# Four more weight slots for the experts, the overflow branch moved to their middle, and the forgetting attention as a pipeline over pairs of heads

## The chip, the cores and the metric

The kernel runs on one core of a Trainium2 chip. The metric is device time in microseconds (us); lower is better. "PE" is TensorE, "DVE" VectorE, "ACT" ScalarE, "POOL" GpSimd and "SP" the engine whose queue issues nearly all loads of weights.

## What is computed

Two transformer blocks over 256 tokens of width 1024, all in float32: first a mixer of latent attention and retention, cross attention to a memory, and a mixture of experts (MoE); then a mixer of forgetting attention ("fox") and pooling, a SwiGLU, an RWKV7 mixer and a second SwiGLU. The change touches the MoE and the fox mixer:

```python
# MoE: 32 experts, 2 of a chosen group of 8 per token
a = jnp.einsum('sd,edf->sef', hr, w_gate)
u = jnp.einsum('sd,edf->sef', hr, w_up)
act = jax.nn.silu(a) * u * gate[:, :, None].astype(hr.dtype)
return jnp.einsum('sef,efd->sd', act, w_down)
# fox: 8 heads of 64, query blocks of 128
logits = (jnp.einsum('bhqd,bhkd->bhqk', q_i, k).astype(jnp.float32) * scale
          + c_i[..., :, None] - cum[..., None, :])
p = jax.nn.softmax(jnp.where(causal, logits, -1e30), axis=-1)
return jnp.einsum('bhqk,bhkd->bhqd', p.astype(v.dtype), v)
# ... attn = attn * jax.nn.sigmoid(og), then concatenated with the pool and times w_out
```

## The kernel before, in words

The tokens are two tiles of 128. Each engine runs one straight program; semaphores join them. The PSUM banks are rings (`fill` on PE, `take` on the reader; a fill waits until its bank's last reader is done).

**Weights.** Every load of weights is a "unit" of up to 1 MB in a slot of 2048 floats per partition. SP issues the units strictly in the order in which the program lists them (`stream`, line 297 issues); before one goes out, SP waits until the unit that last held the slot has been used (`released`), and for slots outside `ring_w` also on a fence. There are 13 slots: 0 to 7 are `ring_w`, 8 to 12 lie in `work` from 12288.

**MoE.** Experts come in 8 quads of 4. A quad has 12 units: 4 gate, 4 up and 4 down matrices, 96 units in all, put into the slots in the turn 0-3, 8-12, 4-7. So unit n waits for the use of unit n-13. The fence of slots 8 and up is a transpose late in the cross attention. A chosen token is gathered into 32 places of its expert by a selection matrix (`Sel`, made by DVE, line 1571, for all 8 quads at once; `SelG`, line 1611, is the same times the gate). PE's order for quad q is: gate matmuls of q (line 1337), transposes and down matmuls of q-1 (1352), gather of q+1 (1388), transposes of `SelG` (1398), up matmuls of q (1337 again), scatter of q-1 (1409). Gate slots are free after the gate matmuls, up slots after the up matmuls, down slots after the down matmuls. ACT applies SiLU (1236) and copies the down result (1488); DVE multiplies and adds the scatter to the residual X (1602).

**Overflow.** If an expert got more than 32 tokens, a branch computes the rest densely. PE, ACT, DVE and SP each read a flag and jump over that branch; it stands after the last quad (for SP after the last expert unit is issued). It isn't taken with these inputs.

**Into fox.** `rounded_linear` computes the 2568 columns of `w_fin` in three passes of rounded halves. ACT makes the high half of each unit (`part_high_act`, line 503, 1.9 us a unit), DVE the low half (line 512). ACT does units 0 and 1, normalises token tile 0 (lines 414, 420, with POOL at 425 and 426), does units 2 and 3, normalises tile 1. PE warms up (line 462), transposes tile 0 (441), computes column block 0 of tile 0, transposes tile 1, and goes on.

**Fox attention.** PE computes the scores of all 8 heads (lines 1906, 1908); DVE adds decay and mask (2057) and takes the row maximum by pairs (2062, 2063); ACT takes the exponential by head (1972); PE transposes the probabilities by head (1915), ACT copies them out; then PE computes all outputs with the probabilities stationary and v moving (1924 to 1927), DVE divides by the row sum (2071) and multiplies by the sigmoid gate (2074), PE transposes the result (1933), ACT copies it into `mixT`, and the output projection `w_out2` starts (341). The constant table comes in two loads at the start (lines 578, 592); its `decay` part is last used by the retention (`ro`).

## Time and profile before

| | |
|---|---|
| median of 3 runs | 1367.98 us (1365.78 to 1368.43) |
| profiled execution, its own time | 1374.08 us |
| its span | 1372.2 us |
| PE busy in the span | 1222.1 us (89%) |
| DVE, ACT, POOL busy | 735.2, 247.9, 94.3 us |
| mean granted TensorE clock | 0.946 |
| DMA | 247.25 MB, mean 180 GB/s |

Times below are us from the start of the span. The MoE lies between about 305 and 548, the fox mixer between 548 and 702. In a timeline row the bracket says how long the engine had been idle before and what ended that. "issue" is time in which the engine waited for nothing that the profile shows. PEclk is the granted clock as a share of 2.4 GHz.

### The profile page before, as it was taken

To read this page: it belongs to the slowest core of one execution; us is meant where nothing else is said; L and a number is where in the kernel's file an instruction comes from. 1 tells how busy PE (TensorE), PEld (TensorE's weight loads), DVE (VectorE), ACT (ScalarE), POOL (GpSimd) and SP (SyncE) were. 2 spreads that over 40 slices of the span, in tenths; PEclk is the share of its full clock that TensorE was granted. 3 is DMA by queue.
4 is the path that set the end of the run, shared out by engine and by line. 5 is a ranking of instruction groups with operands and counts; after the bars stand their busy time and mean duration, and the time that the engine had idled before them with its cause. 6 is when DMAs were issued, how large, how long until landed. Compare 5 with 4: busy or idle time off the path is not lost.

```text
span 1372.2 us, 20894 instructions
## 1 busy us (share of the span) xinstructions
PE 1222.1 (89%) x9023; PEld 880.1 (64%) x9023; DVE 735.2 (54%) x1178; ACT 247.9 (18%) x427; POOL 94.3 (7%) x86
## 2 busy tenths in 40 slices
PE   5999998998666668898899999989999898999997
PEld 4855645555333333587558888766769884688886
DVE  5447412142111111555188777677876657777774
ACT  5413111210000001523210000135331100100000
POOL 1010000000000000120000000000110431000000
PEclk9999999999888878999799999999999999999999
DMA  9643243167999999350465553136300224855500
GB/s 345 230 169 123 87 157 123 41 239 308 402 390 408 402 383 394 120 176 1 158 230 185 187 187 127 34 86 223 110 2 4 65 65 161 269 184 184 185 31 31
DMA packets 106338, 247.25 MB, mean 180 GB/s; under 512 B 8113, under 2 KB 56256, under 8 KB 93826
## 3 DMA queue, kind: packets, MB, share of 16 engines
q1 hardware_dynamic: 106052, 245.71, 49.2%
q8 instruction: 73, 1.20, 0.4%
q0 software_dynamic: 144, 0.15, 0.0%
q14 instruction: 23, 0.19, 0.0%
q10 hardware_dynamic: 46, 0.01, 0.0%
HBM read 244.80 MB, written 1.05 MB: 179 GB/s over the span
## 4 chain that ended last, share of the span: by engine, by line
PE 80%; DMA 10%; DVE 4%; ACT 2%; SPq 2%; issue 2%; POOL 0%; DVEq 0%
PE bank L479 13%; PE bank L478 13%; PE bank L480 13%; DMA ring_w<-expert_w_gate 8%; PE bank L341 8%; PE bank L327 6%; PE bank L2332 4%; PE bank L1337 3%; PE bank L1352 2%; SPq L297 1%; PE bank L462 1%; PE bank L2226 1%; PE bank L441 1%; DMA work<-expert_w_down 1%; PE bank L1747 1%
## 5 line engine op out<-in xcount | busy, mean ns | idle before, releaser
L478 PE MATMUL bank<-work_rounded,work_rounded 128*128 128x512 f32 (+2 forms) x704 | 278.1, 395 | 6.8 <-DVE work_rounded L1681 5.2
L480 PE MATMUL bank<-work_rounded,work_rounded 128*128 128x512 f32 (+2 forms) x704 | 275.1, 391 | 0.0
L479 PE MATMUL bank<-ring_w_rounded,work_rounded 128*128 128x512 f32 (+2 forms) x576 | 228.1, 396 | 0.0
L478 PEld LDWEIGHTS bank<-work_rounded,work_rounded 128*128 128x128 f32 x704 | 133.1, 189 | 37.5 <-issue 3.9
L480 PEld LDWEIGHTS bank<-work_rounded,work_rounded 128*128 128x128 f32 x704 | 132.8, 189 | 27.9
L479 PEld LDWEIGHTS bank<-ring_w_rounded,work_rounded 128*128 128x128 f32 x576 | 110.0, 191 | 23.3 <-issue 0.2
L341 PE MATMUL bank<-ring_w,work 128*128 128x512 f32 x256 | 113.4, 600 | 2.6 <-ACT work L1143 1.4
L1681 DVE TENSOR_TENSOR ring_w_rounded<-ring_w,work_rounded 128x1024 fp32r<-128x1024 f32 x84 | 102.9, 1225 | 2.9
L1337 PE MATMUL bank<-ring_w,work 128*32 128x256 f32 x768 | 71.2, 459 | 35.1 <-DMA ring_w<-expert_w_gate 33.0
L1236 ACT ACTIVATE work<-bank 128x256 f32<-128x256 f32 x52 | 20.1, 386 | 406.7 <-PE bank L480 340.3
L341 PEld LDWEIGHTS bank<-ring_w,work 128*128 128x128 f32 x256 | 48.5, 193 | 60.8 <-issue 57.4
L327 PE MATMUL bank<-ring_w,work 128*128 128x512 f32 x192 | 83.5, 593 | 0.9 <-DVE work L451 0.9
L1595 DVE TENSOR_TENSOR work<-bank,cols 128x512 f32<-128x512 f32 x16 | 11.0, 691 | 134.0 <-PE bank L1388 134.0
L479 PE MATMUL bank<-work_rounded,work_rounded 128*128 128x512 f32 x192 | 74.9, 390 | 0.0
L1337 PEld LDWEIGHTS bank<-ring_w,work 128*32 128x32 f32 x768 | 36.4, 131 | 57.4 <-issue 47.6
L1681 DVE TENSOR_TENSOR work_rounded<-work,work_rounded 128x1024 fp32r<-128x1024 f32 (+1 forms) x56 | 64.4, 1149 | 1.9
L327 PEld LDWEIGHTS bank<-ring_w,work 128*128 128x128 f32 x192 | 36.3, 190 | 45.2 <-issue 44.0
L425 POOL TENSOR_SCALAR stat<-stat 128x1 f32<-128x1 f32 (+3 forms) x21 | 7.6, 360 | 767.1 <-ACT work L414 663.4
L1680 DVE CAST work_rounded<-bank 128x256 fp32r<-128x256 f32 x44 | 18.7, 424 | 75.2 <-PE bank L1747 75.2
L1337 PE MATMUL bank<-work 128*32 128x256 f32 x256 | 32.9, 453 | 29.2 <-DMA ring_w<-expert_w_gate 29.2
L1680 DVE CAST work_rounded<-ring_w 128x1024 fp32r<-128x1024 f32 x84 | 57.5, 684 | 0.0
L813 ACT COPY work<-bank 128x512 f32<-128x512 f32 (+3 forms) x53 | 28.3, 559 | 143.1 <-PE bank L480 68.1
(445 smaller groups left out, 1830.6 us busy)
## 6 DMA issues: line engine op xcount, KB each, us to landing
ring_w<-expert_w_gate SPq DMA_DIRECT2D x26, 1024.0 KB, 13.8
ring_w<-expert_w_up SPq DMA_DIRECT2D x22, 1024.0 KB, 19.8
ring_w<-ffn_w_down SPq DMA_DIRECT2D x22, 1024.0 KB, 5.0
work<-expert_w_down SPq DMA_DIRECT2D x20, 1024.0 KB, 9.1
ring_w<-expert_w_down SPq DMA_DIRECT2D x12, 1024.0 KB, 10.5
work<-ffn_w_gate SPq DMA_DIRECT2D x12, 1024.0 KB, 5.5
work<-ffn_w_up SPq DMA_DIRECT2D x12, 1024.0 KB, 8.2
work<-expert_w_up SPq DMA_DIRECT2D x10, 1024.0 KB, 11.5
```

The costliest lines, as they stand in the source:

```text
L327: mm = nc.tensor.matmul(ps[:, 0:w_], lhsT[:, kk, t * P:(t + 1) * P], wv[kk // step][:, kk % step, :], start=kk == 0, stop=kk == kt - 1)
L341: mm = nc.tensor.matmul(ps[:, :], lhsT[:, k, t * P:(t + 1) * P], wv[k // 4][:, k % 4, :], start=k == 0, stop=k == KD - 1)
L478: nc.tensor.matmul(out, lhsT[0], rhs[0], start=first, stop=False)
L479: nc.tensor.matmul(out, lhsT[0], rhs[1], start=False, stop=False)
L480: return nc.tensor.matmul(out, lhsT[1], rhs[0], start=False, stop=last)
L813: nc.scalar.copy(dst, ps[:, 0:dst.shape[1]] if len(dst.shape) == 2 else ps[:, 0:dst.shape[1] * dst.shape[2]].rearrange("p (a b) -> p a b", ...
L1236: nc.scalar.activation(sil[:, i % 2], ps[:, 0:FF], ACT.Silu).then_inc(sem(f"silu_{u}"), 1)
L1337: mm = nc.tensor.matmul(ps[own, i * FF:(i + 1) * FF], hg[:, q % 2, k, own], units_[j][:, k, :], start=k == 0, stop=k == KD - 1)
L1352: mm = nc.tensor.matmul(banks[c][own, :], actT[:, q % 2, k, own], wd[j][:, k, c * 512:(c + 1) * 512], start=k == 0, stop=k == 1)
L1680: links["dve"](nc.vector.tensor_copy(high, value))
L1681: return nc.vector.tensor_tensor(low, value, high.bitcast(F32), ALU.subtract).then_inc(done, 1)
L2332: mm = nc.tensor.matmul(ps[w, h * HD:(h + 1) * HD], lhs(w, 8 * half + h), rhs(w, 8 * half + h), start=True, stop=True)
```

## The change

Four slots are added: 13 and 14 in `work` at 6144 and 8192 (where `Sel` and `SelT` of all quads lay), 15 and 16 over `decay`, `pool` and `sel` of the constant table. The turn becomes 15, 16, 0-3, 8-14, 4-7, so unit n waits for unit n-17. `Sel`, `SelG` and `SelT` shrink to two quads each and are made as the quads go, two ahead. `pool` and `sel` (1.3 MB) are no longer loaded at the start but as `late_const`, after the `w_fin` units. The overflow branch moves to before quad 4 (`MIDDLE`) on PE, ACT and DVE, and for SP to after the last unit of quad 3; ahead of it PE finishes quad 3. At the start of fox, ACT makes the high half of unit 0 only, then normalises tile 0, then does units 1, 2, 3, then tile 1. The fox attention is interleaved by pairs of heads: probabilities are divided by the row sum before they are transposed, v is stationary and the transposed probabilities move, so the output comes out transposed, and the gate is transposed before its sigmoid (`ogT`). Its core:

```diff
-        SLOT, SLOTS, MORE = 2048, 8, 5
+        SLOT, SLOTS, MORE = 2048, 8, 9
...
             if slots[0] < SLOTS:
                 name, base, at = "ring_w", ring_w, slots[0] * SLOT
+            elif slots[0] < 13:
+                name, base, at = "work", work, EXTRA + (slots[0] - SLOTS) * SLOT
+            elif slots[0] < 15:
+                name, base, at = "work", work, 6144 + (slots[0] - 13) * SLOT
             else:
-                name, base, at = "work", work, EXTRA + (slots[0] - SLOTS) * SLOT
+                name, base, at = "const", const, CONST["decay"][0] + (slots[0] - 15) * SLOT
...
+                if (slots[0] >= SLOTS and name != "late_const") or name.startswith("f1"):
+                    late = fence.get(name.split(".")[0], ()) if slots[0] < 15 else ("ro.1",)
...
-        n_const1 = CONST["invf"][1]
+        n_const1, n_const2 = CONST["decay"][1], CONST["sel"][1]
...
-            sp.dma_start(const[:, n_const1:], A["const_table"][:, n_const1:]).then_inc(sem("const2_in"), 16)
+            sp.dma_start(const[:, n_const2:], A["const_table"][:, n_const2:]).then_inc(sem("const2_in"), 16)
...
-        Sel = view(6144, T, NE, CAP)
-        SelT = view(8192, NQ, S)
-        SelG = view(22528, T, NE, CAP)
+        Sel = [view(22528 + 256 * i, T, EPQ, CAP) for i in range(2)]
+        SelG = [view(23040 + 256 * i, T, EPQ, CAP) for i in range(2)]
+        SelT = [view(23552 + 256 * i, S) for i in range(2)]
...
-            turn = itertools.cycle((0, 1, 2, 3, 8, 9, 10, 11, 12, 4, 5, 6, 7))
+            turn = itertools.cycle((15, 16, 0, 1, 2, 3, 8, 9, 10, 11, 12, 13, 14, 4, 5, 6, 7))
...
+            def second_half(q):
+                tr_pe(pe, "moe", q, pick=lambda k: slice(k, FF, 2))
+                down_quad_pe(pe, q)
             for q in range(NQ + 1):
+                if q == MIDDLE:
+                    second_half(q - 1)
+                    scatter(q - 1)
+                    overflow_pe(pe)
                 if q < NQ:
                     await_moved(pe, f"hg.{q}.1")
                     ps = fill(pe, "GU", f"moe.gu.{q}")
                     gu_quad_pe(pe, q, 0, ps)
-                if q:
-                    tr_pe(pe, "moe", q - 1, pick=lambda k: slice(k, FF, 2))
-                    down_quad_pe(pe, q - 1)
+                if q and q != MIDDLE:
+                    second_half(q - 1)
                 if q + 1 < NQ:
                     gather(q + 1)
                 if q < NQ:
                     turn_scatter(q)
                     gu_quad_pe(pe, q, 1, ps)
-                if q:
+                if q and q != MIDDLE:
                     scatter(q - 1)
-            drained(pe, "GU", "TT", "Z")
-            drained(pe, "Y")
-            if "O" in phases:
-                overflow_pe(pe)
+            drained(pe, "GU", "TT", "Z", "Y")
...
+            def select(q):
+                if q >= 2:
+                    peek(dve, f"hg.{q - 2}.1")
+                V.tensor_tensor(Sel[q % 2], slots_of(key, q), each, ALU.is_equal).then_inc(sem("selected"), 1)
+            def weigh(q):
+                dve.wait_ge(sem("selected"), q + 1)
+                if q >= 2:
+                    peek(dve, f"selT.{q - 2}")
+                V.tensor_tensor(SelG[q % 2], Sel[q % 2], slots_of(gate, q), ALU.mult).then_inc(sem("gated"), 1)
+            select(0)
+            select(1)
...
+                if q == MIDDLE:
+                    add_scatter(q - 1)
+                    overflow_dve(dve)
                 if q + 1 < NQ:
                     take_gather(q + 1)
                 if q < NQ:
+                    if q + 2 < NQ:
+                        dve.wait_ge(sem("gated"), q + 1)
+                        select(q + 2)
+                    if q + 1 < NQ:
+                        weigh(q + 1)
                     ps = take(dve, "Z", f"selT.{q}")
-                    V.tensor_copy(SelT[:, q], ps[:, 0:S]).then_inc(moved["Z"], 1)
+                    if q >= 2:
+                        peek(dve, f"x.{q - 2}.1.1")
+                    V.tensor_copy(SelT[q % 2], ps[:, 0:S]).then_inc(moved["Z"], 1)
                     step_dve(dve, "moe", q)
-                if q:
+                if q and q != MIDDLE:
                     add_scatter(q - 1)
...
+            place("late_const", (15, 16), [(A["const_table"][:, n_const1:n_const2], const[:, n_const1:n_const2])])
...
+            def pair_outputs(p):
+                ps = fill(pe, "D", f"foT.{p}")
+                for i in range(2):
+                    h, own = 2 * p + i, slice(i * HD, (i + 1) * HD)
+                    await_moved(pe, f"fprT.{h}")
+                    nc.tensor.matmul(ps[own, 0:S], v(0, h), fprT[:, h, 0:S], start=True, stop=False)
+                    mm = nc.tensor.matmul(ps[own, P:S], v(1, h), fprT[:, h, S:3 * P], start=False, stop=True)
                 mm.then_inc(full["D"], 1)
-            for h in range(FH):
-                pe.wait_ge(sem("fexp"), 2 * h + 2)
-                ps = fill(pe, "A", f"fprT.{h}")
-                for b in range(3):
-                    mm = nc.tensor.transpose(ps[:, b * P:(b + 1) * P], fsc[:, h, b * P:(b + 1) * P], ident)
-                mm.then_inc(full["A"], 1)
-            await_moved(pe, f"fprT.{FH - 1}")
-            v = lambda t, h: fproj[:, t, 2 * FW + h * HD:2 * FW + (h + 1) * HD]
-            for t in range(T):
-                ps = fill(pe, "D", f"fo.{t}")
-                for h in range(FH):
-                    o = slice(h * HD, (h + 1) * HD)
-                    if t == 0:
-                        mm = nc.tensor.matmul(ps[:, o], fprT[:, h, 0:P], v(0, h), start=True, stop=True)
-                    else:
-                        nc.tensor.matmul(ps[:, o], fprT[:, h, P:S], v(0, h), start=True, stop=False)
-                        mm = nc.tensor.matmul(ps[:, o], fprT[:, h, S:3 * P], v(1, h), start=False, stop=True)
-                mm.then_inc(full["D"], 1)
-            for t in range(T):
-                pe.wait_ge(sem("fgated"), t + 1)
-                ps = fill(pe, "A", f"foT.{t}")
-                for k in range(4):
-                    mm = nc.tensor.transpose(ps[:, k * P:(k + 1) * P], fo[:, t, k * P:(k + 1) * P], ident)
-                mm.then_inc(full["A"], 1)
+            pair_scores(0)
+            pair_scores(1)
+            pair_turned(0)
+            pair_scores(2)
+            pair_outputs(0)
+            pair_turned(1)
+            pair_scores(3)
+            for p in range(1, 4):
+                pair_outputs(p)
+                if p < 3:
+                    pair_turned(p + 1)
...
-            out_linear(pe, "w_out2", mixT, lambda t: await_moved(pe, f"foT.{t}"), lambda: norm_pe(pe, "f0", tiles=(0,)))
+            out_linear(pe, "w_out2", mixT, lambda t: await_moved(pe, "foT.3"), lambda: norm_pe(pe, "f0", tiles=(0,)))
...
-            if "C" in phases:
-                peek(act, f"selT.{NQ - 1}")
             part_high_act(act, "w_fin", 0)
-            part_high_act(act, "w_fin", 1)
             def ready(t):
                 if t:
-                    part_high_act(act, "w_fin", 2)
-                    part_high_act(act, "w_fin", 3)
-                if "C" in phases:
-                    await_moved(act, f"x.{NQ - 1}.1.{t}")
+                    peek(act, f"x.{NQ - 1}.1.1")
+                    for n in (1, 2, 3):
+                        part_high_act(act, "w_fin", n)
+                await_moved(act, f"x.{NQ - 1}.1.{t}")
...
-            await_moved(act, "w_fin.3.0", "w_fin.3.1")
-            og = fproj[:, :, OG:OG + FW]
-            nc.scalar.activation(og, og, ACT.Sigmoid).then_inc(sem("fgate"), 1)
...
-                if h:
-                    copy_chunk_act(act, f"fprT.{h - 1}", fprT[:, h - 1])
-            copy_chunk_act(act, f"fprT.{FH - 1}", fprT[:, FH - 1])
-            for t in range(T):
-                ps = take(act, "A", f"foT.{t}")
-                nc.scalar.copy(mixT[:, 0:4, t * P:(t + 1) * P], ps[:, :].rearrange("p (k n) -> p k n", k=4)).then_inc(moved["A"], 1)
+            act.wait_ge(sem("fss"), T)
+            for t in range(T):
+                ps = take(act, "A", f"ogT.{t}")
+                nc.scalar.activation(gateT[:, :, t * P:(t + 1) * P], ps[:, :].rearrange("p (k n) -> p k n", k=4),
+                                     ACT.Sigmoid).then_inc(moved["A"], 1)
...
+                if p:
+                    pair_turned_act(p - 1)
...
             part_low_dve(dve, "w_fin", 0)
+            norm_split_dve(dve, "d", "mix_norm_2", 0)
             part_low_dve(dve, "w_fin", 1)
-            norm_split_dve(dve, "d", "mix_norm_2", 0)
             part_low_dve(dve, "w_fin", 2)
...
+            def pair_probs_dve(p):
+                pair = slice(2 * p, 2 * p + 2)
+                dve.wait_ge(sem("fexp"), 4 * p + 4)
+                L(V.reciprocal(fst[:, 6:8, pair], fst[:, 6:8, pair]))
                 for t, (lo, hi) in enumerate(((0, P), (P, 3 * P))):
-                    last = V.scalar_tensor_tensor(fsc[:, h, lo:hi], ps[:, lo:hi], cum[:, t, h:h + 1], C("cmask")[:, lo:hi],
-                                                  ALU.add, ALU.add)
-                last.then_inc(moved["D"], 1)
-                if h % 2:
-                    await_moved(dve, f"fscore.{h}")
-                    L(V.tensor_reduce(fst[:, 4, h - 1:h + 1], fsc[:, h - 1:h + 1, 0:P], AX.X, ALU.max, negate=True))
-                    V.tensor_reduce(fst[:, 5, h - 1:h + 1], fsc[:, h - 1:h + 1, P:], AX.X, ALU.max, negate=True) \
-                        .then_inc(sem("fnmax"), 1)
-            dve.wait_ge(sem("fexp"), 2 * FH)
-            L(V.reciprocal(fst[:, 6:8, 0:FH], fst[:, 6:8, 0:FH]))
-            dve.wait_ge(sem("fgate"), 1)
-            for t in range(T):
-                ps = take(dve, "D", f"fo.{t}")
-                v = fo[:, t].rearrange("p (h d) -> p h d", h=FH)
-                V.tensor_tensor(v, ps[:, :].rearrange("p (h d) -> p h d", h=FH), bc(fst[:, 6 + t, 0:FH], HD, 2),
-                                ALU.mult).then_inc(moved["D"], 1)
-                await_moved(dve, f"fo.{t}")
-                V.tensor_tensor(fo[:, t], fo[:, t], fproj[:, t, OG:OG + FW], ALU.mult).then_inc(sem("fgated"), 1)
+                    V.tensor_tensor(fsc[:, pair, lo:hi], fsc[:, pair, lo:hi], bc(fst[:, 6 + t, pair], hi - lo, 2),
+                                    ALU.mult).then_inc(sem("fprob"), 1)
+            def pair_gated_dve(p):
+                ps = take(dve, "D", f"foT.{p}")
+                V.tensor_tensor(mixT[:, p, :], ps[:, 0:S], gateT[:, p, :], ALU.mult).then_inc(moved["D"], 1)
+            pair_scores_dve(0)
+            pair_scores_dve(1)
+            pair_probs_dve(0)
+            pair_scores_dve(2)
+            pair_probs_dve(1)
+            await_moved(dve, "ogT.1")
+            pair_gated_dve(0)
+            pair_scores_dve(3)
+            pair_probs_dve(2)
+            pair_gated_dve(1)
+            pair_probs_dve(3)
+            pair_gated_dve(2)
+            pair_gated_dve(3)
...
-        add_swiglu("E", "f0", 0, lambda act: after_residual(act, "w_out2"), ("fmixed.1", "fo.1"),
+        add_swiglu("E", "f0", 0, lambda act: after_residual(act, "w_out2"), ("fmixed.1", "foT.3"),
...
-            cut = unit_at[f"moe.d.{NQ - 1}.{EPQ - 1}"] + 1 if "C" in phases and "O" in phases else 0
+            cut = unit_at[f"moe.d.{MIDDLE - 1}.{EPQ - 1}"] + 1 if "C" in phases and "O" in phases else 0
```

## Rows read from the trace of the kernel before

**Rows 1.** Waits of PE over the whole span: us in total, times, longest
```profile
PE bank L1337 <- DMA ring_w<-expert_w_gate: 62.2, 7, 10.8
PE bank L462 <- issue: 8.0, 1, 8.0
```
**Rows 2.** The chain that ended last, in order of time: start us, us, what
```profile
315.17 10.35 DMA ring_w<-expert_w_gate
...
527.79 10.09 DMA work<-expert_w_down
538.13 5.34 PE bank L1352 x32
547.29 8.00 issue
```
**Rows 3.** Timeline of SP's issues: start us, us from first issue to last, group
```profile
221.39 8.55 SPq L297 DMA_DIRECT2D ring_w<-expert_w_gate  x4
269.40 2.41 SPq L297 DMA_DIRECT2D work<-expert_w_up  x4
...
285.33 30.27 SPq L297 DMA_DIRECT2D ring_w<-expert_w_gate  x4
...
529.55 56.38 SPq L297 DMA_DIRECT2D ring_w<-hy_w_in  x11
```
**Rows 4.** Windows in the MoE: stretch, busy us by engine, PEclk, DMA share, GB/s
```profile
399.00:400.00 1.00, 1.00 (x16) 0.22 (x8) 0.00 (x0) 0.38 (x1) 0.00 (x0) 1.00 0.31 115
400.00:401.00 1.00, 1.00 (x10) 0.67 (x7) 0.00 (x0) 0.54 (x1) 0.00 (x0) 1.00 0.14 57
...
314.00:540.00 226.00, 156.69 (x1516) 85.48 (x1512) 35.59 (x62) 14.23 (x30) 0.00 (x0) 0.84 0.96 393
...
404.00:424.00 20.00, 11.53 (x112) 5.42 (x114) 4.20 (x7) 0.38 (x1) 0.00 (x0) 0.79 1.01 425
```
**Rows 5.** Timeline of PE in the MoE: start us, us, line, shape
```profile
310.61 3.66 PE L1337 MATMUL bank<-ring_w,work 128*32 128x256 f32 x64 [1.96 <-issue]
314.20 3.84 PE L1388 MATMUL bank<-work 128*128 128x128 f32 x32
...
343.14 3.89 PE L1409 MATMUL bank<-work 128*128 128x512 f32 x8
356.99 5.55 PE L1337 MATMUL bank<-ring_w,work 128*32 128x256 f32 x64 [9.95 <-DMA ring_w<-expert_w_gate]
```
**Rows 6.** Timeline of DVE, ACT and PE from the last expert into the fox part
```profile
547.33 0.69 DVE L1602 TENSOR_TENSOR X<-X,bank 128x512 f32<-128x512 f32 x1 [0.17 <-PE bank L1409]
...
549.72 3.70 ACT L503 CAST work_rounded<-ring_w 128x2048 fp32r<-128x2048 f32 x2 [5.61 <-issue]
...
556.72 1.15 ACT L420 ACTIVATE work<-X,stat 128x1024 f32<-128x1024 f32 x1 [2.25 <-POOL stat L426]
...
567.87 1.03 PE L441 MATMUL bank<-const,work 128*128 128x128 f32 x8
```
**Rows 7.** Timeline of PE and DVE in the fox attention
```profile
640.71 0.60 PE L1906 MATMUL bank<-work 128*128 128x256 f32 x2
...
659.09 3.68 PE L1924 MATMUL bank<-work 128*128 128x64 f32 x16 [0.57 <-ACT work L813]
...
671.10 1.12 PE L1933 MATMUL bank<-const,work 128*128 128x128 f32 x4 [0.66 <-DVE work L2074]
...
648.85 1.53 DVE L2057 SCALAR_TENSOR_TENSOR work<-bank,work,const 128x128 f32<-128x128 f32 x4
650.41 0.42 DVE L2062 TENSOR_REDUCE work<-work 128x2 f32<-128x256 f32 x1
650.87 0.69 DVE L2063 TENSOR_REDUCE work<-work 128x2 f32<-128x512 f32 x1
```
**Rows 8.** Windows of the fox attention, columns as in Rows 4
```profile
635.00:640.00 5.00, 1.55 (x11) 1.26 (x10) 3.70 (x6) 0.00 (x0) 0.00 (x0) 1.00 0.01 3
...
655.00:660.00 5.00, 3.61 (x14) 2.42 (x14) 0.25 (x1) 3.41 (x13) 0.00 (x0) 0.50 0.00 0
```

More of the change, by code:

```diff
@@ L78, in _constants @@
     parts["sel"] = sel.reshape(P, -1)
+    parts["tri"] = (i[:, None] <= i[None, :]).astype(float)
+    parts["ones"] = np.ones((P, P))
     blk = i // CH
@@ L1569, in moe_dve @@
             each = slot_key.unsqueeze(1).unsqueeze(1).to_broadcast([P, T, EPQ, CAP])
-            for q in range(NQ):
-                V.tensor_tensor(quad(Sel, q), slots_of(key, q), each, ALU.is_equal).then_inc(sem("selected"), 1)
+            def select(q):
[9 more added lines that the diff above has]
+            select(1)
             V.tensor_copy(place_of, by_tile).then_inc(moved["D"], 1)
@@ L1608, in moe_dve @@
                                   bc(gate8[:, t], G, 1), ALU.mult))
-            dve.wait_ge(sem("selected"), NQ)
-            for q in range(NQ):
-                V.tensor_tensor(quad(SelG, q), quad(Sel, q), slots_of(gate, q), ALU.mult).then_inc(sem("gated"), 1)
+            weigh(0)
             await_moved(dve, "rank", "count")
@@ L1929, in fox_pe @@
[L1929 to L1934 removed]
+            for t in range(T):
+                ps = fill(pe, "A", f"ogT.{t}")
+                for k in range(4):
+                    mm = nc.tensor.transpose(ps[:, k * P:(k + 1) * P], fproj[:, t, OG + k * P:OG + (k + 1) * P], ident)
+                mm.then_inc(full["A"], 1)
@@ new lines, in fox_pe, with pair_scores @@
+            await_moved(pe, "fT.1.1")
+            def pair_scores(p):
+                for h in (2 * p, 2 * p + 1):
+                    ps = fill(pe, "D", f"fscore.{h}")
+                    for t, (lo, hi) in enumerate(((0, P), (P, 3 * P))):
+                        nc.tensor.matmul(ps[:, lo:hi], fqz[:, h, t * P:(t + 1) * P], fkT[:, h // 2, 0:hi - lo],
+                                         start=True, stop=False)
+                        mm = nc.tensor.matmul(ps[:, lo:hi], C("sel")[:, h * P:(h + 1) * P], ncumT[:, 0:hi - lo],
+                                              start=False, stop=True)
+                    mm.then_inc(full["D"], 1)
```

131 lines of the change are left out of this document (74 added, 57 removed).

## Prediction, before the changed kernel was run

> **What bounds the kernel now.** I read the waits of PE first. Seven waits of the expert gate matmuls for their weights make 62.2 us, and one single wait of 8.0 us at line 462 is put down to "issue" [rows 1]; nothing else on PE comes near. The chain in order of time puts both on the path that sets the end: transfers of expert weights (first row at 315.17), the last expert transfer until 537.9, its down matmuls, the scatter, and then 8.00 us in which nothing runs [rows 2]. So the MoE is bound by DMA, and the rest of the kernel by PE.
>
> Next, why the transfers take so long. The SP timeline shows four gate units at 221.39, nothing until the fence opens at 269.40, and a group of four that begins at 285.33 and ends 30.27 us later: its last three wait until quad 0's gate matmuls end at 314.27 [rows 3, 5]. So 13 units are there when the MoE begins and 83 are not. In the windows a stretch without holes moves 425 GB/s, while 399 to 401 moves 115 and 57, and the whole of 314 to 540 averages 393 [rows 4]. 226 us at 393 GB/s is 88.8 MB; at 425 this would take 209 us. So about 17 us of it are holes, some 2.4 us in each of seven quads. They come from the slots: the down units of quad q sit where those of q-1 sat (n-13), and these are freed only by the down matmuls of q-1, which PE does after the gate matmuls of q. When gate q lands, only up q (4 units, 4 x 2.47 = 9.9 us, 1.049 MB at 425 GB/s being 2.47 us) is queued; gate matmuls 5.55 [rows 5], transposes, ACT's copy and down matmuls take about 11 together.
>
> **Part 1: four slots more.** (a) 17 units are there before the MoE, 79 are not: 4 x 2.47 = 9.9 us less to move while PE waits. Slots 15 and 16 have an open fence, slots 8 to 14 open at 269.40: seven units and then the ring's four are 11 x 2.47 = 27.2 us, in by 297, before the first gate matmuls at 310.61 [rows 3, 5]. (b) With n-17, the down units of q wait for gate q-1 and up q-1, and gate q+1 for up q-1 and down q-1. When gate q lands, nine units (22 us) are queued, and down q-1 ends after 11: no hole. For the ramp: from 314.3, units 17 to 20 go out at once (10 us), the next four after up 0, near 322, the next after down 0, near 332; each comes before the one ahead is through. PE needs per quad 5.5 gate, 5.3 down, 3.8 gather, 3.7 up, 3.9 scatter [rows 2, 5] and about 1 of transposes, 23 us of the 29.6 that 12 units take, so PE doesn't become the bound. Sum: 9.9 + 17 = 27 us at best. I take 25.5, since a hole at the ramp or in the middle may remain. The floor is (a) with a third of the holes closed, 15 us; the ceiling adds about 1 us because DVE makes 2 selections instead of 8 ahead of the first gather's copy, 28 us.
>
> The Trainium skill, "DMA: Bandwidth & Descriptors", section Specifications, says that HBM gives one core some 358 GB/s. By that the 79 units would take 231 us and this part would lose time instead of gaining. The trace speaks against it for this kernel: 425 GB/s over 20 us [rows 4].
>
> The new waits in DVE's loop (selections of q+2 behind gather q, `SelT` behind the scatter of q-2) cost two short operations per quad, beside DVE that is idle most of the MoE (35.59 us busy of 226 [rows 4]): nothing. If PE ever waited for them it would be under 1 us a quad. The two constant parts that go later (1.3 MB, 3 us of queue) stand behind `w_fin` and are needed 65 us after it begins; they push the pool and output weights by 3 us, which lie ready for tens of us. SP issues one load more: nothing. At the start PE has no wait that this load ends: nothing.
>
> **Part 2: the branch leaves the end.** Before, the scatter ends at 547.3 and PE's next matmul is 8.00 us later [rows 2]; ACT loses 5.61 and then makes two high halves (3.70) before the normalisation [rows 6]. After: ACT ends its copy of the down result near 544.1 and does high half 0 until 546.0, tile 0 of X is complete at 546.1, square 1.2, POOL 2.25, scale 1.15 [rows 6]: transposes at 550.9 where they were at 558.9, 8 us gained. Then it gives some back: ACT does three high halves (5.6) instead of two ahead of tile 1, and DVE one low half (2.3) more inside the critical part. Tile 1 is normalised at 561.0; PE ends column block 0 at about 560.1 and waits 0.9. Its transposes of tile 1 start at 561 where they were at 567.87 [rows 6]: 6.5 us net. Ceiling 8; floor 3, if DVE's low halves (2.3 each) let PE wait once more.
>
> The branch isn't gone: in the middle PE finishes quad 3 and then loses the same 8 us. From the landing of down 3 (T): down 5.3, copy, scatter 3.9, branch 8, gate 4 until about T+23, gather and up 4 until T+32; gate 5 lands at T+39.6. The nearest slot that depends on gate 4 is wanted at T+42. So it is covered, with 7 us to spare.
>
> **Part 3: the fox attention.** Before, it goes from 638.85 (scores) to 672.2 (output projection). PE: a head's scores 1.3 us, as a 128x256 product takes 0.43 from start to start at full clock [rows 7]; outputs 10.2 us, at half clock. In the pipeline the loop is DVE scores of p (after PE's last head: 0.75 of 1.53, then 0.42 and 0.69 [rows 7]), DVE division (no such row; as reductions of the same sizes, plus the reciprocal, 1.5), PE transposes of p-1 (0.9), PE scores of p+1 (2.6), DVE again: 2.1 + 1.5 + 0.9 + 2.6 = about 7.3 with hops, twice after 646.2, so the last scores stand at 660.8. Two more divisions, ACT's exponentials and copies, transposes and the last output pair end near 669 at full clock. Output pairs with v stationary are 2 x (0.43 + 0.22) = 1.3 us; the row of the old form, 3.68 for 16, bounds it from above at 2.6 [rows 7]. But PE will wait about half the time. In the row 635 to 640 it was busy 1.55 of 5 us and the clock stayed at 1.00 (2.4 GHz); in 655 to 660, after a stretch of waits, it was 0.50 (1.2 GHz) [rows 8]. At half clock from 655 on, scores, transposes and outputs double and the end is 676. Between 669 and 676 I take 671: 1 us gained (bounds +3 and -4). The gate's transposes fill PE's wait for DVE before 638.85 and ACT's two sigmoids come well before the first exponential: nothing; without that cover 2 us.
>
> **Sum:** 25.5 + 6.5 + 1 = 33 us. The profiled execution took 1374.08 us (span 1372.2), 6.1 above the median of 1367.98; it becomes 1341, and the median 1335.
>
> **Rivals.**
> A. The holes stay in part: PE's releases come late again (half-clock matmuls, or SP's queue doesn't take 13 units ahead), and only the head start and a few us are won. For it: SP waits in order, one late slot holds up all behind. Against: nine units of cover. 11 + 5 + 0 = 16: 1352 us.
> B. The branch in the middle shows. SP also jumps there, and while it does, nothing is issued; PE loses its 8 us while it already has the reordered quad. Against: at SP's end-of-MoE jump only about 1.4 us passed before the first `w_fin` unit at 529.55 [rows 3], and 11 units are in flight then. Price 8: 1343 us. The Trainium skill, "Runtime: NRT & Kernel Launch", section Instruction fetch mechanics, says that a jump outside the fetched pages stalls for a fetch; it would put such a stall on every engine with the branch.
> C. The fox pipeline is slower than the old order (half clock from 650, every hop exposed): it loses 5 us instead of gaining 1, so 1341 us.
> D. Slower than before: PE stays at half clock through the whole MoE, because it never gets a long busy stretch. Then a quad is gate 5.5, up 5.5, down 5.3, gather 7.5, scatter 7.7, transposes 2: 34 us against 31.8 now and 29.6 of DMA. PE is then the bound, from any quad cost over 29.6 on; it decides the sign only over about 35, including a branch and hops. At 36, 8 x 4.2 = 34 lost and 7 won elsewhere: 1395 us. Against: the mean clock of 314 to 540 is 0.84 with longer waits than the new ones [rows 4].
> E. The change doesn't do what it says, say a fence holds slots 13 to 16: then part 2 and 3 alone, 1360 us.
>
> **Chances.** Forecast 0.70, A 0.13, B 0.05, C 0.05, D 0.03, E 0.04. A measurement of this kernel can tell 0.2% (2.7 us) from no change. Faster needs over 2.7 of the 33 us: all but D, a bad A and a bad E: 0.94; within 0.2%: 0.02; slower: 0.04. The three ceilings, 28 + 8 + 3 = 39 us, give 1329; I go 4 us beyond, for terms set to nothing that may give something (1325). Upward the range ends at A's 1352, which leaves out D, E and the worse half of A.
>
> **What would show it.** Right: 17 expert units issued before the first gate matmul; windows of 420 to 425 GB/s without a hole from 315 to about 510; PE's waits on expert weights of about 7 us each; last expert unit landed near 511; an "issue" wait of 8 us between quads 3 and 4 and none at line 462; gap from landing to tile 1's transposes 23 instead of 30 us; from fox's first score to the output projection about 32 us. Wrong: a period per quad above 30.5 us, PE waiting on DVE's selections, or a granted clock of 0.5 in most of the fox attention.

## The result, and the profile after

The changed kernel takes **1336.49 us** (median of 4 runs; three of them lie between 1335.52 and 1336.51, the fourth, 4686.64 us, was disturbed), the kernel before 1368.2 us beside it (1365.78 to 1370.8, 4 runs). The ratio is **0.9766, 95% interval 0.9743 to 0.9788**: 31.7 us less. The forecast was 1335.0 in a range of 1325 to 1352.

| | before | after |
|---|---|---|
| profiled execution, its own time | 1374.08 us | 1335.52 us |
| its span | 1372.2 us | 1333.7 us |
| PE busy | 1222.1 us | 1201.3 us |
| mean granted TensorE clock | 0.946 | 0.967 |
| DMA | 247.25 MB | 247.27 MB |

Both spans are cut here at the same five places: the first gate matmul, the last down matmuls (their weights have then landed), tile 1's transposes, the first fox score and the first matmul of `w_out2`. All later experiments are cut at these places too.

| stage, us | before | after | less |
|---|---|---|---|
| start to first gate matmul | 310.6 | 306.7 | 3.9 |
| MoE, to the landing of the last weights | 227.5 | 206.8 | 20.7 |
| to the transposes of tile 1 | 29.7 | 22.3 | 7.4 |
| `w_fin`, to the first fox score | 71.0 | 71.5 | -0.5 |
| fox attention, to `w_out2` | 33.2 | 30.5 | 2.7 |
| `w_out2` to the end | 700.2 | 695.8 | 4.4 |

The four stages in the middle give 30.3 us. In the first and the last stage I know of nothing that the change could shorten, and yet they differ by 8.3; the experiments come back to this.

**The MoE.** The longer waits of PE from 300 to 540: us in total, times, longest. They answer to [rows 1].

```profile
PE bank L1342 <- DMA work<-expert_w_gate: 21.2, 3, 9.0
PE bank L1342 <- DMA ring_w<-expert_w_gate: 16.1, 2, 8.6
PE bank L1342 <- issue: 9.1, 3, 7.5
...
PE bank L1357 <- DMA work<-expert_w_down: 3.6, 1, 3.6
PE bank L466 <- DVE X L1627: 1.0, 1, 1.0
```

Seven waits of 62.2 us are now five waits of 37.3, about 7.5 each, and the wait at the warm-up matmuls (line 466, which was 462) went from 8.0 to 1.0. The "issue" wait of 7.5 is the branch in its new place. Next, windows with columns as in [rows 4]:

```profile
310.00:514.00 204.00, 150.94 (x1508) 81.89 (x1504) 39.45 (x71) 14.23 (x30) 0.00 (x0) 0.88 1.01 415
325.00:345.00 20.00, 15.70 (x150) 9.06 (x146) 5.56 (x10) 0.97 (x2) 0.00 (x0) 0.91 1.01 422
...
405.00:425.00 20.00, 13.92 (x162) 8.66 (x162) 2.81 (x6) 0.38 (x1) 0.00 (x0) 0.83 1.01 411
...
485.00:505.00 20.00, 12.17 (x152) 5.99 (x156) 0.91 (x2) 1.54 (x3) 0.00 (x0) 0.83 1.02 422
```

The last two columns are DMA share and GB/s. No stretch looks like the two rows of 115 and 57 GB/s of before: the transfers run through, and eight of the nine 20 us windows from 325 to 505 lie between 419 and 422. That is a little under the 425 of [rows 4]. The Trainium skill, "DMA: Bandwidth & Descriptors", section Measured, gives 425 GB/s for a long load while the other core of the pair is idle, beside the lower limit of its Specifications; the rows here side with the measured figure.

SP's timeline (start, us from first issue to last, group) shows the head start; it answers to [rows 3]:

```profile
196.88 1.11 SPq L301 DMA_DIRECT2D const<-expert_w_gate  x2
218.60 0.81 SPq L301 DMA_DIRECT2D ring_w<-expert_w_gate  x2
226.34 0.81 SPq L301 DMA_DIRECT2D ring_w<-expert_w_up  x2
266.62 0.81 SPq L301 DMA_DIRECT2D work<-expert_w_up  x2
267.47 2.63 SPq L301 DMA_DIRECT2D work<-expert_w_down  x4
270.14 0.46 SPq L301 DMA_DIRECT2D work<-expert_w_gate  x1
274.43 8.07 SPq L301 DMA_DIRECT2D ring_w<-expert_w_gate  x3
282.56 0.42 SPq L301 DMA_DIRECT2D ring_w<-expert_w_up  x1
310.45 0.81 SPq L301 DMA_DIRECT2D const<-expert_w_up  x2
...
501.99 52.14 SPq L301 DMA_DIRECT2D ring_w<-hy_w_in  x11
```

2 + 2 + 2 + 2 + 4 + 1 + 3 + 1 = 17 units go out before the MoE, and the 18th at 310.45, when quad 0's gate matmuls (306.74 to 310.40) end.

**The branch.** PE in the middle of the MoE:

```profile
397.57 3.89 PE L1414 MATMUL bank<-work 128*128 128x512 f32 x8
408.92 0.65 PE L1342 MATMUL bank<-ring_w,work 128*32 128x256 f32 x3 [7.46 <-issue]
...
432.62 5.84 PE L1342 MATMUL bank<-work 128*32 128x256 f32 x64 [8.98 <-DMA work<-expert_w_gate]
```

The stall stands between the scatter of quad 3 and the gate matmuls of quad 4, and PE still waits 9.0 us for the weights of quad 5: the stall is covered with 9 us to spare (7 were forecast). The chain in order of time at the end of the MoE, answering to [rows 2, 6]:

```profile
485.06 28.26 DMA work<-expert_w_down
513.57 6.31 PE bank L1357 x32
519.88 1.93 PE bank L1414 x4
...
522.55 1.16 ACT work L418 x2
...
525.70 5.49 ACT work_rounded L507 x3
...
534.63 1.16 ACT work L424
535.84 1.09 PE bank L445 x8
```

Landing, down matmuls, half a scatter, normalisation: the one idle time of size between them is an "issue" wait of 1.04 us on ACT, before its high halves. Tile 0's transposes start 12.9 us after the landing (526.48 in PE's timeline; 20.7 before), tile 1's 22.3 after it. The gap narrows again because of ACT's three high halves (5.49), as forecast.

**The fox attention.** PE's and DVE's timelines, answering to [rows 7]:

```profile
617.69 1.29 PE L1961 MATMUL bank<-const,work 128*128 128x128 f32 x6 [3.16 <-DVE work L2125]
...
626.01 0.87 PE L1961 MATMUL bank<-const,work 128*128 128x128 f32 x6 [2.35 <-DVE work L2125]
...
632.66 0.87 PE L1961 MATMUL bank<-const,work 128*128 128x128 f32 x6 [2.35 <-DVE work L2125]
```

```profile
616.60 1.03 DVE L2125 TENSOR_TENSOR work<-work 128x256 f32<-128x256 f32 x2
621.58 0.74 DVE L2113 SCALAR_TENSOR_TENSOR work<-bank,work,const 128x128 f32<-128x128 f32 x2 [3.95 <-PE bank L1952]
...
628.23 0.74 DVE L2113 SCALAR_TENSOR_TENSOR work<-bank,work,const 128x128 f32<-128x128 f32 x2 [1.94 <-PE bank L1952]
```

They read as a loop between the two engines: PE idles 3.16 and 2.35 us until DVE has divided, then transposes and computes the next scores, and DVE idles 3.95 and 1.94 us until it has those. From one transposes row to the next 8.3 and 6.7 us pass (7.3 was forecast). And the clock did not fall far. These are the whole attention before and after, and the same of a kernel of experiment 2 with the same attention (columns as in [rows 4]):

```profile
638.85:672.01 33.16, 28.01 (x144) 24.59 (x145) 13.11 (x29) 10.89 (x41) 0.00 (x0) 0.73 0.03 7
```

```profile
607.35:637.88 30.53, 21.44 (x121) 17.28 (x121) 16.34 (x40) 11.51 (x41) 0.00 (x0) 0.89 0.00 0
```

```profile
612.55:645.75 33.20, 24.43 (x120) 19.38 (x121) 16.34 (x40) 11.60 (x41) 0.00 (x0) 0.79 0.00 0
```

In the old form PE was busy 28.0 of 33.2 us at a mean clock of 0.73, and from 655 on, in slices of 5 us, the clock was 0.50 ([rows 8] has the first). The pipeline has PE busy for 21.4 us, idle for 9.1, and at a mean clock of 0.89; in slices of 5 us it never shows less than 0.66. How long the pipeline takes goes with that clock: 28.6 to 28.8 us at 0.94 (four traces), 30.5 at 0.89 (two), 33.2 at 0.79 (one).

### The profile page after: what moved, and what is told of

Same layout as the page of the kernel before. It is cut to its first block, busy times and chain, and to the rows that moved or that the text cites. A ratio compares the mean times of both kernels' runs of the same rounds, so it can differ in the third digit from the quotient of the medians.

```text
span 1333.7 us, 20901 instructions
## 1 busy us (share of the span) xinstructions
PE 1201.3 (90%) x9007; PEld 860.1 (64%) x9007; DVE 737.7 (55%) x1189; ACT 246.7 (18%) x426; POOL 93.4 (7%) x86
## 2 busy tenths in 40 slices
DMA packets 106484, 247.27 MB, mean 185 GB/s; under 512 B 8130, under 2 KB 56273, under 8 KB 93971
## 4 chain that ended last, share of the span: by engine, by line
PE 75%; DMA 9%; DVE 9%; ACT 3%; SPq 2%; issue 2%; POOL 1%; DVEq 0%
PE bank L483 13%; PE bank L482 13%; PE bank L484 13%; PE bank L345 8%; PE bank L331 6%; DMA work<-expert_w_gate 5%; PE bank L2402 4%; PE bank L1342 3%; DMA work<-expert_w_down 2%; PE bank L1357 2%; SPq L301 2%; DMA ring_w<-expert_w_gate 1%; PE bank L1393 1%; PE bank L445 1%; PE bank L1084 1%
## 5 line engine op out<-in xcount | busy, mean ns | idle before, releaser
L1342 PE MATMUL bank<-ring_w,work 128*32 128x256 f32 x512 | 52.3, 431 | 32.3 <-DMA ring_w<-expert_w_gate 16.1
L1342 PEld LDWEIGHTS bank<-ring_w,work 128*32 128x32 f32 x512 | 26.4, 123 | 50.9 <-issue 44.1
L1342 PE MATMUL bank<-work 128*32 128x256 f32 x384 | 39.0, 443 | 13.3 <-DMA work<-expert_w_gate 13.3
```

The lines of the kernel that those rows point to most:

```text
L1342: mm = nc.tensor.matmul(ps[own, i * FF:(i + 1) * FF], hg[:, q % 2, k, own], units_[j][:, k, :], start=k == 0, stop=k == KD - 1)
```

## The experiments

The kernels of the first four experiments were run in one set (kernel before in it: 1367.77 us, 9 runs), the next four in a second (1366.59, 11 runs), the last three in a third (1371.3, 11 runs). Ratios are to the kernel before of the same set.

**1. Only 13 slots again, everything else kept.**

```diff
-            turn = itertools.cycle((15, 16, 0, 1, 2, 3, 8, 9, 10, 11, 12, 13, 14, 4, 5, 6, 7))
+            turn = itertools.cycle((0, 1, 2, 3, 8, 9, 10, 11, 12, 4, 5, 6, 7))
```

> The changed kernel with the old turn of 13 slots; all else of the change stays. If the slots bring the gain of the MoE by a head start of four units (9.9 us) and by closing the holes of some 2.4 us a quad (17 us at most), this kernel takes back 21 to 27 us: 1358 to 1363 us, with holes again in the stream and a last expert unit that lands 21 to 27 us later than in the changed kernel. If only the head start counts, it is 10 us slower: 1346 us.

Measured: 1358.43 us, ratio 0.9939 (0.9912 to 0.9966). Waits of PE, and a window of the kernel with 13 slots:

```profile
PE bank L1342 <- DMA ring_w<-expert_w_gate: 54.4, 6, 10.9
...
340.00:500.00 160.00, 106.07 (x1024) 57.00 (x1022) 28.94 (x52) 9.66 (x20) 0.00 (x0) 0.84 0.98 403
```

The holes are back (403 GB/s), and the MoE takes 224.9 us. By the medians the four slots are worth 1358.4 - 1336.5 = 22 us, by the MoE stage of the two traces 224.9 - 206.8 = 18.1; 57 to 69% of the whole gain. That the head start alone counts (1346 us) is ruled out.

**2. 15 slots: without the two in the constant table.**

```diff
-            turn = itertools.cycle((15, 16, 0, 1, 2, 3, 8, 9, 10, 11, 12, 13, 14, 4, 5, 6, 7))
+            turn = itertools.cycle((0, 1, 2, 3, 8, 9, 10, 11, 12, 13, 14, 4, 5, 6, 7))
```

> The changed kernel with 15 slots (the two over the constant table unused). The slot theory counts what is queued when gate q lands: 7 units, 17 us, against 11 us until the down matmuls of q-1 are done, so no hole is left, and only two units of the head start are lost: 5 us slower, 1341 to 1342 us, with DMA at 420 GB/s throughout. If each slot gives an equal share, it loses half of what 13 slots lose: 11 to 13 us, 1348 us.

Measured: 1341.35 us, ratio 0.981 (0.9776 to 0.9843), MoE 210.5 us. Its window, and the same of the changed kernel:

```profile
340.00:500.00 160.00, 107.53 (x1022) 57.79 (x1020) 28.47 (x51) 9.63 (x20) 0.00 (x0) 0.84 1.01 420
```

```profile
340.00:500.00 160.00, 113.65 (x1102) 60.96 (x1106) 27.47 (x49) 10.00 (x21) 0.00 (x0) 0.85 1.01 420
```

So 15 slots already close the holes, and the last two bring only their head start: 4.9 us by the medians, 3.7 in the stage, for two units of 2.5. The steps are 17 us for slots 13 and 14 (14.4 in the stage) and 5 for slots 15 and 16. By my estimate from this step, a further slot would be worth about 2.5 us; no run has one.

**3. The branch back at the end, everything else kept.**

```diff
             for q in range(NQ + 1):
-                if q == MIDDLE:
-                    second_half(q - 1)
-                    scatter(q - 1)
-                    overflow_pe(pe)
...
             drained(pe, "GU", "TT", "Z", "Y")
+            overflow_pe(pe)
```

(the same on ACT and DVE, and for SP behind the last expert unit)

> The changed kernel with the overflow branch back after the last quad, on all four engines. If its 8 us of issue time stand on the path there and are hidden in the middle: 6.5 to 8 us slower, 1343 to 1344.5 us, and the issue wait of 8 us is again ahead of line 466. If the end of the MoE is set by ACT and POOL anyway: under 3 us slower.

Measured: 1339.29 us, ratio 0.9794 (0.9754 to 0.9835; 4 runs). PE's timeline has the stall where it was:

```profile
512.12 5.34 PE L1357 MATMUL bank<-work 128*32 128x512 f32 x32 [2.03 <-DMA work<-expert_w_down]
517.39 3.89 PE L1414 MATMUL bank<-work 128*128 128x512 f32 x8
529.30 2.93 PE L466 MATMUL bank<-const 128*128 128x512 f32 x3 [8.03 <-issue]
```

From landing to tile 1's transposes 29.9 us pass instead of 22.3: the 7.6 of the theory. The time, though, rose by 2.8 only, less than the 6.5 to 8 expected, with wide intervals. That number is the rival's (under 3 us), but the rival's reason, that ACT and POOL set the end of the MoE anyway, does not fit the 7.6 us in the stage. Experiment 10 repeats it.

**4. No branch at all.** Since it isn't taken with these inputs, nothing that runs is left out but the reading of the flag and the jump.

```diff
         def overflow(eng, body):
-            eng.wait_ge(sem("flags"), 1)
-            some = eng.value_load(flags[0:1, 0:1], min_val=0, max_val=1)
-            with eng.If(some > 0):
-                body()
+            return
```

> The changed kernel without the overflow branch at all (with these inputs the branch isn't taken, so nothing is left out that runs). If the branch in the middle is fully hidden by the transfers: no change, 1335 to 1337.5 us. If it shows: up to 8 us faster, 1328.5 us.

Measured: 1336.35 us (4 runs from 1333.05 to 1343.04), ratio 0.9792 (0.9746 to 0.9838), MoE 205.4 us against 206.8, and against 205.5 in a second trace of the changed kernel (experiment 9). PE in the middle of it:

```profile
398.65 0.42 PE L1342 MATMUL bank<-ring_w,work 128*32 128x256 f32 x3
...
428.11 5.16 PE L1342 MATMUL bank<-work 128*32 128x256 f32 x64 [16.19 <-DMA work<-expert_w_gate]
```

PE goes on at once behind the scatter (398.65, no idle time in front), and then waits 16.2 us for quad 5 instead of 9.0. The stall was a part of a wait: the wait is longer by 7.2 us where the stall of 7.46 is gone. In the middle the branch costs nothing that these runs can show.

**5. The old fox attention in the changed kernel.** All of the fox part on PE, ACT and DVE is as before; slots, branch and order of the halves are as after.

```diff
-            pair_scores(0)
-            pair_scores(1)
-            pair_turned(0)
...
+            for h in range(FH):
+                ps = fill(pe, "D", f"fscore.{h}")
...
-            out_linear(pe, "w_out2", mixT, lambda t: await_moved(pe, "foT.3"), lambda: norm_pe(pe, "f0", tiles=(0,)))
+            out_linear(pe, "w_out2", mixT, lambda t: await_moved(pe, f"foT.{t}"), lambda: norm_pe(pe, "f0", tiles=(0,)))
```

> The changed kernel with the forgetting attention in the old order (all scores, all transposes, all outputs, division and gate at the end). The forecast's term for the pipeline is 1 us, the two traces say 2.7 us from the first score to the output projection (33.2 against 30.5): 1337.5 to 1339 us. If the pipeline is worth its full-clock sum: 1339.5 us; if it costs time at half clock: 1333 us.

Measured: 1340.7 us, ratio 0.9799 (0.9772 to 0.9826). The attention takes 34.8 us against 30.5, 4.3 less in the pipeline. In the whole time it is 4.2 by the medians and 3.6 by the means of these six runs and of nine of the changed kernel, all but the one of 4686.64 (1340.8 and 1337.2), somewhat more than expected. In the old order PE's timeline has the outputs of all heads in one block, behind the last head's exponential and copy. The clock is 1.00 from 613 to 623 and 0.50 from 628 on, so this block and the transposes behind it run at half clock:

```profile
630.09 3.67 PE L1961 MATMUL bank<-work 128*128 128x64 f32 x16 [0.57 <-ACT work L817]
```

**6. The scores two pairs ahead.** If the ring of hops between PE and DVE is the limit, PE has to compute the scores of pair 2 before it waits for the division of pair 0.

```diff
             pair_scores(1)
-            pair_turned(0)
             pair_scores(2)
+            pair_turned(0)
             pair_outputs(0)
-            pair_turned(1)
             pair_scores(3)
+            pair_turned(1)
```

> The changed kernel with PE's order in the fox pipeline altered: scores of pair 2 before the transposes of pair 0, scores of pair 3 before the transposes of pair 1. In the changed kernel DVE waits 3.95 us for the scores of pair 2 and 1.94 us for those of pair 3, since PE first waits for the probabilities. If that hop bounds the pipeline: 5 to 7 us from the first score to the output projection, 1330 to 1331.5 us. If DVE or ACT bound it, or the clock does: under 2 us.

Measured: 1332.94 us, ratio 0.9733 (0.9704 to 0.9763). The attention takes 23.9 us: 6.6 less, as the theory said. PE's waits for the divided probabilities (us in total, times, longest), in the changed kernel and in this one, give 6.3 of it:

```profile
PE bank L1961 <- DVE work L2125: 7.9, 3, 3.2
```

```profile
PE bank L1961 <- DVE work L2125: 1.6, 2, 1.0
```

The median fell by 3.6 only, to above the 1330 to 1331.5 expected; see experiment 11.

**7. The same, with six filler matmuls of 256 columns in PE's waits, to hold the clock.**

```diff
+            FILL = (2, 2, 2, 0)
...
+                        for _ in range(FILL[p]):
+                            nc.tensor.matmul(ps[:, 0:256], ident, const[:, 0:256], start=True, stop=True)
```

> As scores_ahead, and PE fills its waits for the probabilities with two idle products of 128x256 each before the transposes of pairs 0 to 2. If the half clock in this stage costs time once the order is right: 1 to 3 us faster than scores_ahead. If PE is busy enough by then, or its time is covered by DVE: no change, or up to 1 us slower where a product runs into the wait's end.

Measured: 1332.15 us, ratio 0.9726 (0.9696 to 0.9757): 0.8 below experiment 6, well inside the intervals. The attention takes 24.7 us. The mean granted clock of the attention is 0.93 in both, and 1.00 behind its first 5 us, so there was no low clock for the fillers to lift. They are not worth having.

**8. The kernel before once more, for its trace.** Its one run of 1368.24 us has a span of 1366.4.

> The kernel before, unchanged, for a second trace of it. The first trace was 6 us above the median and differs from the changed kernel's by 3.9 us before the first gate matmuls, where the change does next to nothing. If that is the variation of single executions, this trace has its first gate matmuls at 305 to 311 us and a span of 1362 to 1372 us, and its MoE and fox stages as long as in the first trace (227.5 and 33 us, within 3 us).

| stage, us | before | again | after | 3 | 4 | 1 | 2 |
|---|---|---|---|---|---|---|---|
| to the first gate matmul | 310.6 | 308.6 | 306.7 | 306.4 | 303.9 | 305.0 | 309.7 |
| MoE | 227.5 | 225.1 | 206.8 | 205.7 | 205.4 | 224.9 | 210.5 |
| fox attention | 33.2 | 33.2 | 30.5 | 28.8 | 28.7 | 30.5 | 33.2 |
| `w_out2` to the end | 700.2 | 699.2 | 695.8 | 698.0 | 699.7 | 699.3 | 700.2 |

(The numbers in the head are those of the experiments.) The second trace came out as expected, but its MoE is 2.4 us shorter than in the first, so against it the slots gain 18.3 us in the stage and not 20.7. The MoE follows the slots. The first stage varies from 303.9 to 309.7 among kernels whose PE program is the same there, and the last from 695.8 to 700.2. So the 3.9 and 4.4 us of these stages in the first table can't be told from that variation. The fox attention as a pipeline also takes 28.6 to 33.2 in single traces: over the seven traces that have it (experiments 9 and 10 below among them) the mean is 29.9, against 33.7 over the three of the old form (33.2, 33.2, 34.8), 3.8 us less.

**9, 10, 11. Changed kernel, branch at the end and scores ahead, once more side by side.** They are to settle the two places where a trace shows 7 us and the medians of two sets about 3.

> The changed kernel as it is, measured beside the next two on one chip, because the first medians were taken in two batches and lie within each other's intervals. Theory: 1335 to 1338 us, ratio to the kernel before 0.976 to 0.978. In its trace the MoE phase is 206 to 208 us and the fox attention 30.5; what differs from the first trace lies before the first gate matmul or behind the fox attention.

> The changed kernel with the overflow branch back at the end of the experts. Theory of the branch (it costs 7.5 us at the end and nothing in the middle): 7 to 8 us slower than after_again of this batch, 1343 to 1345. Rival (the stall is partly made up later, so that less than half is left, as the first median of 1339.3 suggests): 2 to 4 us slower. Both theories expect the 8 us issue wait at line 466 in the trace; they differ in the time alone.

> The changed kernel with the scores of pairs 2 and 3 ahead of the transposes of pairs 0 and 1. Theory of hops (6.6 us shorter fox attention, and nothing given back): 5.5 to 7 us faster than after_again of this batch, 1329 to 1331. Rival (half is given back after the attention, as the 3 us longer rest of the first trace suggests): 3 to 4 us faster, and the phase behind the attention again about 3 us longer than that of after_again.

| | us, median (6 runs) | ratio, interval | landing to tile 1 | fox | `w_out2` to end |
|---|---|---|---|---|---|
| 9, changed kernel | 1337.99 | 0.976, 0.9719 to 0.9802 | 21.1 | 28.6 | 700.5 |
| 10, branch at the end | 1339.82 | 0.9792, 0.9749 to 0.9835 | 29.5 | 28.8 | 693.1 |
| 11, scores ahead | 1330.20 | 0.9708, 0.9667 to 0.9749 | 22.0 | 23.9 | 698.8 |

Experiment 9 came out as expected, but its MoE (205.5) and its attention (28.6) are a little shorter than the ranges said. Experiment 11 is 7.8 us below 9, and its last stage is 1.7 shorter, not 3 longer: these traces show nothing that is given back. With the runs of before, 12 of this kernel stand against those 9 of the changed kernel: 1332.8 against 1336.5 by median, 1331.4 against 1337.2 by mean, so about 4 to 6 us. The attention itself is 4.7 to 6.6 shorter. This version beats both kernels.

Experiment 10 stays 1.8 us above 9, where the theory wanted 7 to 8 and the rival 2 to 4; over both sets it is 1340.2 against 1337.2 by mean, 3.0 us, each mean uncertain by about 1 (standard error of 10 and of 9 runs). Its trace has the stall in full:

```profile
512.52 5.23 PE L1357 MATMUL bank<-work 128*32 128x512 f32 x32 [2.42 <-DMA work<-expert_w_down]
...
529.56 3.60 PE L466 MATMUL bank<-const 128*128 128x512 f32 x4 [7.99 <-issue]
```

From the landing to the first fox score the two traces with the branch at the end take 100.9 and 100.5 us, the two of the changed kernel 93.8 and 93.7: 7 us are still there. To `w_out2` it is 129.7 and 129.3 against 124.3 and 122.4: 5 to 7 us. The rest of the span is then 698.0 and 693.1 against 695.8 and 700.5, some 2.6 shorter. Part of that is the clock: from 926 to 946, and again from 966 to 986, the trace of experiment 9 has a granted clock of 0.83 where experiment 10 has 1.00, with PE equally busy. The first stretch in 9, then in 10:

```profile
926.00:946.00 20.00, 20.00 (x84) 15.62 (x83) 14.64 (x20) 10.44 (x12) 0.00 (x0) 0.83 0.30 106
```

```profile
926.00:946.00 20.00, 20.00 (x97) 15.56 (x96) 11.00 (x13) 12.23 (x12) 0.00 (x0) 1.00 0.51 180
```

Whether a kernel that idled for 8 us at 520 is granted a better clock 400 us later, or whether two traces are too few, these runs don't tell. What is shown is the stage: moving the branch shortens it by 7 to 8 us, and 7 of them last until the first fox score. That 3 to 5 of these are missing in the whole time is measured, but not explained.

## Why the prediction was right, and where its terms were off

**Slots: forecast 25.5 us, bounds 15 to 28; measured 20.7 in the stage (18.1 and 18.3 by two other pairs of traces), 22 by the medians of experiment 1.** The mechanism was right point by point: 17 units ahead of the MoE, no holes, last weights landed at 513.3 (511 forecast), PE not the bound. The sum 9.9 + 17 was too big in both terms. The step that was off is "226 us at 393 GB/s is 88.8 MB; at 425 this would take 209 us. So about 17 us of it are holes": the 226 us of 314 to 540 include the time before the first transfer (chain: 315.17) and after the last expert unit had landed (537.9). In the 222.7 us between, the trace moved 395 GB/s, or 88.0 MB, for which 425 GB/s would need 207.0 us; that leaves holes of 15.7, 1.3 less. The stream without holes was taken at 425 GB/s, the value of one 20 us window; the changed kernel's transfers took 201.9 us (from 311.4, a microsecond after SP's first issue at 310.45, to the landing at 513.3) at 418 GB/s, and their 84.4 MB would have taken 198.6 at 425: 3.3 less. And 88.0 - 84.4 = 3.6 MB are 8.5 us at 425, not the 9.9 of four units, 1.4 less; the bytes that are no expert units make the difference, and whose they are I did not trace. 27 - 1.3 - 3.3 - 1.4 = 21.0 is near the 20.8 by which the transfers became shorter. Rival A (the holes stay in part) did not happen; experiment 2 shows that even 15 slots leave none.

**Branch: forecast 6.5 us; measured 7.4 in the stage (7.6 against experiment 3, 8.4 in the pair of experiments 9 and 10), of which the whole time shows about 3.** Tile 0's gain of 8 was 7.8 (20.7 against 12.9 from the landing), and the give-back ahead of tile 1 was 0.4 instead of the 1.5 forecast. The stall in the middle was covered with 9 us against 7. Rival B (it shows in the middle) is ruled out by the traces of experiment 4: the stall is there on PE with 7.46 us, but within a wait that is longer. A stall at the jump is what "Runtime: NRT & Kernel Launch" of the Trainium skill (section Instruction fetch mechanics) says of a jump outside the fetched pages. The trace agrees in so far as the instruction queues carry 4 packets from 403 to 410, within the stall, and none there in experiment 4; how the 7.46 us divide between the fetch and the reading of the flag, no run tells, since experiment 4 takes out both. That the last 3 to 5 us of the stage's gain are missing in the time stays open.

**Fox attention: forecast 1 us, between 669 at full clock and 676 at half; measured 2.7 in the two traces, 3.8 over all of them, and 4.2 in the time against experiment 5.** The hop arithmetic held (7.3 per pair against 8.3 and 6.7). The step that was off is "At half clock from 655 on, scores, transposes and outputs double", and with it the choice of 671: over the seven traces the attention takes 29.9 us, which from 638.85 ends at 668.7, at the full-clock bound of 669. The 3.8 us lie above the ceiling of +3. PE's waits of 2 to 3 us between bursts did not pull the clock down for long (0.89 and 0.94 in the mean), though in one trace of seven it was 0.79 and the whole gain was gone (33.2 us). A row of the old attention, in which PE was busy 3.61 of 5 us at 0.50, was a poor guide to the new one. Rival C (slower) fell with it.

**The rest.** `w_fin` took 0.5 more: nothing, as said. Rival D (PE at half clock through the MoE) saw a clock of 0.88 instead of 0.84, the other way. Rival E falls by the 17 units and experiment 1.

**The sum** of 33 against 31.7 is nearer than its parts. In the traces 20.7 + 7.4 + 2.7 - 0.5 = 30.3. By undoing single parts: 22 + 3 (experiments 3 and 10) + 4 = 29. The slots were put 3.5 to 7 too high, the fox attention 2 to 3 too low, and the branch was right in its stage and 3 too high in the time. That the total came within 1.5 us of the forecast is in part luck.

## What to carry to other kernels

Count what is queued at the moment in which a consumer starts, and compare it with the time until the consumer gives the next slot back: 4 units of 2.5 us against 11 us of work left a hole in each round; 7 units (15 slots) left none. Past that point the next two slots were worth only about the transfer time of what they held ahead of the stage, 2.5 us each, so measure the slots by stage before you fight for more. When a loop between two engines idles both in turn, as 2 to 3 us on PE and 2 to 4 on DVE did here, move the producer one step further ahead in its own order: moving two calls by one place each gave 4.7 to 6.6 us of the stage, where the whole pipeline had given about 4. And when such a loop varies from one execution to the next, look at its granted clock before you look for a cause in the program: 28.6 us at 0.94 and 33.2 at 0.79 were the same attention.

## What was not expected of the hardware

- With a long queue the stream ran at 419 to 422 GB/s in eight of nine 20 us windows, one per cent under the 425 of a short window before. And SP itself seems to be held back: in the chain of waits its issues take 2.07 to 2.08 us each, where the chain of the kernel before has 0.33 to 0.48 for most. The load at 396.93 goes into slot 11, whose last user, an up matrix of quad 3, PE had finished at 389.44. What holds SP, no run tells.

```profile
392.58 2.08 SPq L301
...
396.93 2.08 SPq L301
```

- A branch that isn't taken, with the reading of its flag, holds PE for 8.0 us at the end (7.99 and 8.03), 7.5 in the middle, and ACT for 5.6. SP jumps too, behind the last unit of quad 3: 1.4 us pass there, from 366.65 to its next issue at 368.02, and the window from 365 to 385 still moved 421 GB/s. The one low window, 405 to 425 with 411 GB/s, lies at PE's stall instead: in the six traces with the branch in the middle and 17 slots it moved 410 to 416, with the branch at the end 419 and 420, without a branch 422. That is about half a microsecond of transfers. In the stall two instruction queues are at work beside the weights (`--dma`, 403 to 410: packets, MB, share of 16 engines):

```profile
q8 instruction: 2, 0.03, 2.7%
q14 instruction: 2, 0.02, 1.0%
```

ACT's row in experiment 10:

```profile
523.98 1.90 ACT L507 CAST work_rounded<-ring_w 128x2048 fp32r<-128x2048 f32 x1 [5.57 <-issue]
```

- Kernels with the same program on PE there take 303.9 to 309.8 us for the first stage, and 693 to 701 for the last. Two single traces can't be compared by their spans to better than some 5 us; stages that the change touches can, to about 2 in the MoE (205.4 to 207.3 over nine traces with 17 slots, 225.1 and 227.5 for the kernel before).
